# Five norm stages in a transformer-like trunk: the last square goes straight to the column means, reciprocals are spread by transposes, and the last projection unit runs by token halves

## The reference

```
def rmsnorm(x, g):
    xf = x.astype(jnp.float32)
    y = xf * lax.rsqrt(jnp.mean(xf * xf, axis=-1, keepdims=True) + EPS)
    return (y * g.astype(jnp.float32)).astype(x.dtype)

def modulate(h, shift, scale):
    return h * (1 + scale[:, None, :]) + shift[:, None, :]

x = x + 0.5 * g1 * swiglu(modulate(rmsnorm(x, norm_g[0]), sh1, sc1))
x = x + g2 * hybrid_mixer(modulate(rmsnorm(x, norm_g[1]), sh2, sc2))
x = x + 0.5 * g3 * swiglu(modulate(rmsnorm(x, norm_g[2]), sh3, sc3))
y = modulate(rmsnorm(x, final_norm_g), shf, scf)
```

## Time and profile before

| | |
|---|---|
| time, median of 3 runs | 1637.83 us (1637.02 to 1642.2) |
| profiled execution, its own time | 1636.69 us |
| profiled execution, span of the trace | 1634.8 us |
| PE busy | 1562.2 us (96%) |
| DVE busy | 728.8 us (45%) |
| ACT busy | 470.9 us (29%) |
| POOL busy | 77.7 us (5%) |
| mean granted TensorE clock | 0.969 of full speed |

### The profile page before, as it was taken

How to read it: one execution, slowest core, us unless ns; L and a number is a source line. 1 busy time by engine, 2 the same in 40 slices (tenths; PEclk the granted TensorE clock), 3 DMA queues, 4 the chain that set the end, 5 groups by cost and what they waited for, 6 DMA issues and landing times.

```text
span 1634.8 us, 26752 instructions
## 1 busy us (share of the span) xinstructions
PE 1562.2 (96%) x10720; PEld 1481.7 (91%) x10720; DVE 728.8 (45%) x927; ACT 470.9 (29%) x642; POOL 77.7 (5%) x139
## 2 busy tenths in 40 slices
PE   7899999999999979999999999997999999999996
PEld 4699999999999969988778999996999999999995
DVE  1622332223322665657776565656222432343245
ACT  4422212221122243544424452224222122212223
POOL 1300000000000030000010000003000000000003
PEclk7799999999999979999999999998999999999996
DMA  8353444534442212231053221222543222222222
GB/s 282 108 155 116 141 128 129 154 116 142 128 129 68 74 43 65 65 108 39 29 167 104 70 69 54 78 73 60 155 136 103 69 73 77 77 77 64 74 68 64
DMA packets 257573, 160.59 MB, mean 98 GB/s; under 512 B 6270, under 2 KB 255290, under 8 KB 257526
## 3 DMA queue, kind: packets, MB, share of 16 engines
q1 hardware_dynamic: 255878, 154.53, 32.3%
q0 software_dynamic: 1648, 5.41, 0.9%
HBM read 151.89 MB, written 8.03 MB: 98 GB/s over the span
## 4 chain that ended last, share of the span: by engine, by line
PE 87%; DVE 6%; DMA 2%; ACT 2%; POOL 1%; issue 1%; SPq 1%; DVEq 0%; ACTq 0%; POOLq 0%
PE acc L593 76%; PE pC L659 3%; DMA ada_raw<-in_w_ada 1%; DVE tmp L1329 1%; DVE hn_lo L1346 1%; PE pB L674 1%; PE pC L821 1%; PE pB L812 1%; POOL tms L542 1%; PE acc L876 1%; PE pC L887 1%; PE pC L620 1%; PE pB L628 1%; PE pC L920 1%; DVE hn_lo L1348 1%
## 5 line engine op out<-in xcount | busy, mean ns | idle before, releaser
L593 PE MATMUL acc<-hn_hi,whi 128*128 128x320 f32 x2128 | 503.3, 318 | 18.8 <-DVE hn_lo L1348 16.0
L593 PE MATMUL acc<-hn_lo,whi 128*128 128x320 f32 x2128 | 487.4, 310 | 0.0
L593 PE MATMUL acc<-hn_hi,wlo 128*128 128x320 f32 x2128 | 487.4, 310 | 0.0
L593 PEld LDWEIGHTS acc<-hn_hi,whi 128*128 128x128 f32 x2128 | 355.6, 190 | 41.7 <-issue 36.5
L593 PEld LDWEIGHTS acc<-hn_lo,whi 128*128 128x128 f32 x2128 | 358.7, 189 | 0.0
L593 PEld LDWEIGHTS acc<-hn_hi,wlo 128*128 128x128 f32 x2128 | 358.1, 189 | 0.0
L1292 DVE TENSOR_TENSOR wlo<-wraw,whi 128x1024 fp32r<-128x1024 f32 (+1 forms) x189 | 226.9, 1201 | 268.1 <-ACT whi L988 261.4
L988 ACT ACTIVATE whi<-wraw 128x1024 fp32r<-128x1024 f32 (+1 forms) x189 | 195.2, 1033 | 166.8 <-PE acc L593 158.7
L593 PE MATMUL acc<-hid_hi,whi 128*128 128x320 f32 x704 | 161.9, 311 | 0.0
L593 PE MATMUL acc<-hid_hi,wlo 128*128 128x320 f32 x704 | 160.3, 308 | 0.0
L593 PE MATMUL acc<-hid_lo,whi 128*128 128x320 f32 x704 | 160.2, 308 | 0.0
(11 more groups left out here) (233 smaller groups left out, 1199.6 us busy)
## 6 DMA issues: line engine op xcount, KB each, us to landing
wraw<-in_ffn_w SPq DMA_DIRECT2D x120, 512.0 KB, 3.8
sraw<-in_w_ada SPq DMA_DIRECT2D x28, 1024.0 KB, 5.1
wraw<-in_w_in SPq DMA_DIRECT2D x37, 512.0 KB, 3.8
ada_raw<-in_w_ada SPq DMA_DIRECT2D x8, 1024.0 KB, 11.1
wraw<-in_w_out SPq DMA_DIRECT2D x16, 512.0 KB, 3.8
sraw<-in_w_ada_final SPq DMA_DIRECT2D x8, 1024.0 KB, 5.5
wraw<-in_ffn_w SPq DMA_DIRECT2D x16, 384.0 KB, 3.4
h0s<-in_state_ssm SPq DMA_DIRECT2D x8, 512.0 KB, 4.8
```

The lines of the kernel that those rows point to most:

```text
L593: last = mm(acc[p][:, h * BANK:h * BANK + HALF], w[:, k, :], a[:, k * TOK + h * HALF:k * TOK + (h + 1) * HALF], start=(k == 0 and t == 0), ...
```

## The change

What it does, part by part:

1. **Last square.** In norms 1, 3 and 4 the square of the eighth x tile is no longer added to `ssum` by DVE. PE takes the means in two steps that add up in PSUM: five products with `ssum` (seven squares), then five with the last square itself.
2. **Spread by transposes.** In all five norms DVE's diagonal matrices and the product with ones go. PE transposes each column of reciprocals, read 128 times over (`broadcast_to`), against the identity: five transposes, the sample columns first. ACT copies in two pieces: 128 sample columns, then 512.
3. **Last unit by halves.** In the last unit before norms 1, 3 and 4 PE does all products of the first token half, counts `half_done`, then those of the second. DVE gates and adds half 0 while PE works on half 1; ACT squares each half. DVE's low part of the next weights stands between the two halves.
4. **POOL.** `norm_samples` multiplies with the scale first and waits for r only before its second instruction. POOL clears `ssum` for norms 0, 1 and 3 (DVE did).
5. **Root table.** ACT loads the table for the root ahead of the last FFN part's down units, by a one-element root; before, it was loaded behind the last square.
6. **High part of the second next weights** (`hi(U_DT + 1)`, `hi(U_F1 + 1)`) goes from before the last square to after the root.
7. **Convolution rows.** `st_row` and `stT` get a place in SBUF above the FFN's tiles, the load is issued before the first FFN, and PE's 12 products stand before `two_units(U_DT)`.

```diff
@@ tensor engine
+        def unit_by_halves(n, i, hi, lo, k_ready):
+            p, kt = n % 2, unit_tiles(n, i)
+            wh, wl = kxn(whi[p], kt, P), kxn(wlo[p], kt, P)
+            pe.wait_ge(wlo_done, i * 2 + (n + 1))
+            wait(pe, acc_free[p], i + n // 2)
+            for h in range(2):
+                for k in range(kt):
+                    if h == 0:
+                        k_ready(k)
+                    for t, (w, a) in enumerate(((wh, hi), (wh, lo), (wl, hi))):
+                        last = mm(half(acc[p], h), w[:, k, :], a[:, k * TOK + h * HALF:k * TOK + (h + 1) * HALF],
+                                  start=(k == 0 and t == 0), stop=(k == kt - 1 and t == 2))
+                if h == 0:
+                    last.then_inc(half_done, 1)
+            last.then_inc(unit_done, 1)
@@ mean_square, spread_r
-            pe.wait_ge(sq_added, (m + 1) * KD)
+            j = LAST_SQUARE.get(m)
+            pe.wait_ge(sq_added, ADDED0[m] + KD - (j is not None))
             for c in range(TT):
-                last = mm(out[:, c:c + 1], ssum[:, c * P:(c + 1) * P], ones_mean[:, 0:1], start=True, stop=True)
+                last = mm(out[:, c:c + 1], ssum[:, c * P:(c + 1) * P], ones_mean[:, 0:1],
+                          start=(c == 0), stop=(j is None and c == ST))
+            if j is not None:
+                for c in range(TT):
+                    if c == 0:
+                        pe.wait_ge(sqhalf_ready, j + 1)
+                    elif c == HALF // P:
+                        pe.wait_ge(sq_ready, (m + 1) * KD)
+                    last = mm(out[:, c:c + 1], sq[:, c * P:(c + 1) * P], ones_mean[:, 0:1], start=False, stop=(c == ST))
...
-            pe.wait_ge(diag_ready, m + 1)
-            for h in range(2):
-                last = mm(pC[:, h * BANK:h * BANK + HALF], ones[:, :], sq[:, h * HALF:(h + 1) * HALF],
-                          start=True, stop=True)
-            last.then_inc(r_mm, 1)
+            pe.wait_ge(rcol_ready, m + 1)
+            for c in (ST, *range(ST)):
+                last = nc.tensor.transpose(pC[:, c * P:(c + 1) * P], rcol[:, c:c + 1].broadcast_to([P, P]), ident[:, :])
+                if c == ST:
+                    last.then_inc(r_tr, 1)
+            last.then_inc(r_tr, 1)
@@ gpsimd, norm_samples
-            pool.wait_ge(rinv_ready, m + 1)
+            pool.wait_ge(rms_mm, m + 1)
+            if m != 4:
+                nc.gpsimd.memset(ssum[:, :], 0.0).then_inc(ssum_zero, 1)
             pool.wait_ge(mod_ready, (1, 2, 2, 2, 3)[m])
...
+                st.done(nc.gpsimd.tensor_tensor(out=tv, in0=by_stream(xT[:, f * TOK + SEQ:(f + 1) * TOK]),
+                                                in1=per_stream[0], op=ALU.mult))
+                if f == 0:
+                    pool.wait_ge(rs_ready, m + 1)
+                st.done(nc.gpsimd.tensor_tensor(out=t[:, :], in0=t[:, :], in1=rT[:, SEQ:TOK], op=ALU.mult))
+                nc.gpsimd.tensor_tensor(out=tv, in0=tv, in1=per_stream[1], op=ALU.add).then_inc(tms_ready, 1)
@@ scalar engine
+        def sqrt_table():
+            A(warm[:, :], eps_t[:, :], ACT.Sqrt)
+        def last_square(m, ready):
+            act.wait_ge(xhalf_ready, LAST_SQUARE[m] + 1)
+            A(half_of(sq, 0), half_of(tile(xT, KD - 1), 0), ACT.Square).then_inc(sqhalf_ready, 1)
+            act.wait_ge(x_ready, ready)
+            A(half_of(sq, 1), half_of(tile(xT, KD - 1), 1), ACT.Square).then_inc(sq_ready, 1)
@@ vector engine
+        def add_gated_by_halves(m, n, q):
+            x = tile(xT, KD - 1)
+            for h in range(2):
...
+                    ins.then_inc(acc_free[n % 2], 1)
+                    evacuated(dve, n)
+                ins = V.tensor_tensor(out=half_of(x, h), in0=half_of(x, h), in1=half_of(xadd, h), op=ALU.add)
+                ins.then_inc(xhalf_ready if h == 0 else x_ready, 1)
+                if h == 0:
+                    lo(n + 1)
...
-            st.done(V.reciprocal(out=rcol[:, :], in_=rcol[:, :]))
-            V.tensor_tensor(out=sq[:, :].rearrange("p (c n) -> p c n", c=TT),
...
+            V.reciprocal(out=rcol[:, :], in_=rcol[:, :]).then_inc(rcol_ready, 1)
```

93 lines of the change are left out of this document (62 added, 31 removed).

## The result

The changed kernel takes 1613.34 us (median of 4 runs, 1611.56 to 1614.74), the kernel before 1637.42 in the same series. The ratio is 0.9846, with a 95% interval of 0.9834 to 0.9857. The forecast was 1614.5. The profiled execution of after took 1614.74 with a span of 1612.9, against a span of 1634.8 before.

The account below looks back on a forecast made before the run. PE was taken as the bound, with gains only where the chain leaves it, mostly five norms: 8.4 + 5.0 + 6.5 + 2.2 + 0.6 = 22.7 us off 1636.69 gives 1614.0; forecast 1614.5, range 1611 to 1617.5.

Parts of the forecast that it names:

- Norm 1, 8.4: Norm 1 gains 8.4 us: loop start 4.9, first tile 0.3, memset 0.6, convolution rows 2.8, less 0.2 for half clock.
- the 5.2 to 5.7 given as its sign: Norm 1: the last unit's end to the loop's first DVE instruction should take 5.2 to 5.7 us.
- sign 2.8: Behind norm 1: the convolution's first unit should come about 2.8 us after norm 1's last products.
- Norm 3, 5.0: Norm 3 gains 5.0 us (4.0 to 5.8): start 4.2 less 0.1 beside POOL, first tile 0.3, memset 0.6.
- the first rival: Half clock reaches last passes and transposes in norms 1, 3, 4: 4.9 us less gain, 1619.4; chance 12%.
- Norm 4, 6.5: Norm 4 gains 6.5 us (5.3 to 6.7), its chain going through POOL's first instruction with r.
- Norm 0, 2.2: Norm 0 gains 2.2 us: spread 1.15, copy 0.1, first tile 0.3, memset 0.6.
- norm 2, 0.6: Norm 2 gains 0.6 us (0 to 0.7) from spread and copy on the way to DVE's loop.
- At nothing: Root's table load, early load of `st_row` and half units were each taken to cost nothing.
- the slower rival (products over one bank): Half units: products must leave their one bank, spacing 0.147 to 0.44 us, 35 us more, 1649; chance 3%.
- the clock drops earlier: Norms 1, 3, 4: half clock reaches the new last passes and transposes, 4.9 us less gain, 1619.4; chance 12%.
- Given back in the loops: Norm loops: POOL's earlier start collides with DVE and loops end as before, 4.9 us less gain, 1619.4; chance 10%.

Follow-up runs that it names:

- i_weights: Changed kernel with high and low part of the second weights of norms 1 and 3 moved ahead of the root: 1612.05 us, ratio 0.9840.
- scaling ahead: Changed kernel where POOL multiplies the sample columns of x by the scale while the last units before norms 1, 3 and 4 run: 1608.04 us.
- u_memset: Changed kernel with the memset of the sum of squares back on DVE, in tile 1 of the norm loops: 1615.12 us, ratio 0.9850.
- u_pool: Changed kernel with POOL's old order in each norm tile, r times x first, so the first tile's instructions wait for r: 1613.26 us, ratio 0.9847.
- comb_nb: Changed kernel with scaling ahead and i_weights together: 1608.18 us, ratio 0.9824.

## Why the prediction was right

Each gain came where it was forecast, and the sum was near: 22.7, against 24.1 between the medians and 21.9 between the two profiled executions. The latter agreement is luck in part, since it rests on two errors that work against each other: the terms were 2.2 too small, and 3.1 went in a stretch that the forecast left alone. Norm 3 gained more than norm 4, the forecast had it the other way round.

- *Norm 1, 8.4; measured 9.5.* The loop started 4.87 after the unit's end, forecast 5.5; this lies outside the 5.2 to 5.7 given as its sign, on the good side, and the term is 5.5 and not 4.9. Weights came last, as forecast. Of the 0.6 that was better, 0.2 is that the second half's gate waited 0.1 for the low part and not 0.3, and 0.2 that the low part did not pay for POOL; the rest lies behind the means, where root, high part and low part took 2.4 and not 2.6. The loop became 1.2 shorter (19.1 to 17.9), forecast 0.9: the first tile gave 0.5, the memset 0.5 and the period 0.7, and the last tile took 0.6 back (1.94 in place of 1.38). What follows the loop became 2.8 shorter, forecast 2.8 less 0.2. PE waits 2.66 behind the two units (sign 2.8), before 5.60, and it ends them 0.2 later behind the loop. By the variant that undoes it, the rows' move was worth 3.1 less the 0.4 that their place ahead of the units costs PE, twice the 0.2 that had been set aside for it.
- *Norm 3, 5.0; measured 6.5.* Start of the loop 5.0 after the unit's end, forecast 5.3. The mis-sized term is the loop: 2.2 shorter where 0.9 stood. The first tile gave 1.0 (3.40 to 2.45) where 0.3 stood, the memset 0.5, and the period, which stood at nothing, 0.7 (five tiles at 2.16 in place of 2.31). The low part and r ended within 0.1 of each other, because the transposes took 1.33 at half clock, the price of the first rival paid in one norm of three and hidden behind the weights.
- *Norm 4, 6.5; measured 6.2.* POOL started with r 3.8 after the unit, forecast 3.7, and so 6.0 earlier than before. The instruction done in advance, up to 0.46 by the forecast, gave 0.1: from POOL's first product with r to the span's end it is 19.56, before 19.69.
- *Norm 0, 2.2, and norm 2, 0.6:* as forecast.
- *At nothing:* half units cost nothing. `L624 x36` took 5.30, 0.147 a product, so the slower rival (products over one bank) falls. The root's table load and the early `st_row` show no wait on the chain; neither they nor the later high part (parts 5 to 7 of the change, but for the place of the 12 products) were undone by themselves.
- *Single parts.* Undone one at a time, spread, direct square, halves, rows and memset give 8.0 + 6.0 + 4.6 + 2.1 + 1.8 = 22.5 us between the medians. By the ratios, which compare series better, it is 18.7 of 25.2. In norms 1, 3 and 4 of the traces (columns to the convolution, to norm 4's T and to the span's end) it is about 25, against the 22.1 that these norms gained. So the parts do not simply add up, and the medians are too coarse to say how. Direct square and halves are worth more than their durations (1.4 each a norm): two norms of three paid 2.3 to 2.6, since their later passes ran at half clock. For the means the rival "the clock drops earlier" did not come true in after: the last six passes ran at full clock in norms 1, 3 and 4 (0.84). In norm 3 of three variants they took 0.97 to 1.14, so this is not sure in each execution.
- *Given back in the loops:* did not happen in norms 1 and 3 of after; in `i_weights` it did.

## What to carry to other kernels

In a chain through all engines, move whatever does not depend on the last result out of it, and give TensorE its part of that work at once: the six passes that were left took 0.84 us, ten that started 0.9 us later took 2.29 in two norms and 1.28 in the third. Where VectorE and GpSimd share a loop, look at which of them waits for the other in each tile; one instruction more at the start of the loop can put them into a slower order for all tiles. And when a term is worth less than the scatter of the medians, read it in the trace between two events around it, as here for the rows and the memset. Set the second event behind the engine that ends last: scaling ahead made two loops 1.2 shorter, and 0.1 of each was left where PE went on.

## What the runs showed of the hardware

- The granted clock at one place differs between traces of kernels whose PE instructions up to there are the same: norm 1's five transposes took 0.76 in after and `u_memset` and 1.33 in `u_pool`, and eight transposes in the mixer 1.09 or 1.97. The times of one kernel scatter by up to 7 us (`comb_nb`: 1606.27 at a granted clock of 0.979, 1613.35 at 0.974).
- Twelve wide products that nobody reads were followed by a stretch at 1.00, where after has 0.50; three of them behind the means, themselves begun when it was falling, were followed by one at 0.51.
- Transposes whose weights are one column, read 128 times, cost no more than others: 0.71 beside running units (1003.52 in after) as in the earlier trace rows.
- A POOL instruction that begins inside a DVE instruction of 1.23 us takes 1.26 in place of 0.45. With POOL and DVE alternating, each of DVE's instructions takes 0.1 to 0.3 longer (L1411 0.85 to 0.99 in place of 0.75). With three POOL instructions a tile the loop's period takes one of two values, 2.16 us where POOL never waits or 2.31 us where it waits 0.23 for DVE in each tile.
